# One order for three units behind each layer norm, and the last head pair scaled like the others

## The reference, cut to what matters

```python
# layer 0: gated short convolution, layer 1: forgetting attention
x = layer_norm(ALPHA * x + y)                      # y: mixer output, x @ w_out or o @ w_o
x = layer_norm(ALPHA * x + (silu(x @ w_g) * (x @ w_u)) @ w_down)
# between the layers, from the same x:
k, v = split(x @ kv_w);  logf = log_sigmoid(x @ f_w + f_b);  q = x @ w_q
# attention, per head: s = q.k/sqrt(64) + C[t] - C[s], causal; p = softmax(s); o = p @ v
```

## Time and profile before

| | us |
|---|---|
| median of 3 runs (2813.22 to 2816.91) | 2814.33 |
| profiled execution, its own time | 2815.04 |
| its span, first to last instruction | 2813.4 |
| TensorE busy in it | 2633.8 (94%) |
| VectorE, GpSimd, ScalarE busy | 1168.8, 840.6, 797.7 |
| mean granted TensorE clock | 0.968 |

### The profile page before, as it was taken

How to read it: one execution, slowest core, us unless ns; L and a number is a source line. 1 busy time by engine, 2 the same in 40 slices (tenths; PEclk the granted TensorE clock), 3 DMA queues, 4 the chain that set the end, 5 groups by cost and what they waited for, 6 DMA issues and landing times.

```text
span 2813.4 us, 44488 instructions
## 1 busy us (share of the span) xinstructions
PE 2633.8 (94%) x16651; PEld 2564.1 (91%) x16651; DVE 1168.8 (42%) x2280; ACT 797.7 (28%) x1491; POOL 840.6 (30%) x500
## 2 busy tenths in 40 slices
PE   8999979999999999878999899888899999999995
PEld 8999968999999999868999788778899999999984
DVE  2222374422222222575255677745532222222247
ACT  3111134111111111253222667632511111111114
POOL 2222244222222222243322666713522222222222
PEclk9999989999999999989999999989899999999996
DMA  3111111111111111104478877621111111111101
GB/s 115 45 45 45 45 32 38 46 46 47 51 47 46 46 46 45 32 23 143 152 263 295 254 209 207 191 72 46 31 46 46 46 46 52 46 46 46 46 31 61
DMA packets 203060, 225.92 MB, mean 80 GB/s; under 512 B 13223, under 2 KB 168871, under 8 KB 201884
## 3 DMA queue, kind: packets, MB, share of 16 engines
q1 hardware_dynamic: 194748, 190.40, 22.0%
q0 software_dynamic: 8160, 33.30, 3.7%
HBM read 182.43 MB, written 41.26 MB: 80 GB/s over the span
## 4 chain that ended last, share of the span: by engine, by line
PE 77%; DVE 10%; issue 4%; DMA 4%; ACT 2%; POOL 2%; SPq 1%; POOLq 0%; DVEq 0%; ACTq 0%
PE ps L2157 24%; PE ps L2158 24%; PE ps L2159 24%; DVE ln_d L1630 2%; DVE ln_t L1688 2%; DVE ln_t L1692 1%; PE ps L2498 1%; DMA o_t<-oe 1%; DMA ncb<-ccum 1%; DVE x L1793 1%; PE ps L2483 1%; PE ps L2480 1%; DVE ln_s L1638 1%; PE ps L2516 1%; ACT ln_y L1130 1%
## 5 line engine op out<-in xcount | busy, mean ns | idle before, releaser
L2157 PE MATMUL ps<-xh,whi 128*128 128x344 f32 x3264 | 1056.2, 324 | 50.5 <-issue 38.9
L2158 PE MATMUL ps<-xl,whi 128*128 128x344 f32 x3264 | 1049.5, 322 | 1.7 <-issue 1.7
L2159 PE MATMUL ps<-xh,wlo 128*128 128x344 f32 x3264 | 1048.7, 321 | 0.0
L765 POOL TENSOR_TENSOR wlo<-wraw,whi 128x1024 fp32r<-128x1024 f32 x196 | 468.3, 2394 | 1604.9 <-ACT whi L1049 1604.8
L2157 PEld LDWEIGHTS ps<-xh,whi 128*128 128x128 f32 x3264 | 619.0, 190 | 61.0 <-issue 44.1
L2158 PEld LDWEIGHTS ps<-xl,whi 128*128 128x128 f32 x3264 | 619.0, 190 | 2.8 <-issue 2.6
L2159 PEld LDWEIGHTS ps<-xh,wlo 128*128 128x128 f32 x3264 | 619.3, 190 | 0.0
L2157 PE MATMUL ps<-zh,whi 128*128 128x344 f32 x1440 | 474.5, 330 | 38.6 <-DVE x L1793 25.0
L1049 ACT ACTIVATE whi<-wraw 128x1024 fp32r<-128x1024 f32 x196 | 206.6, 1056 | 1061.5 <-DMA wraw<-ffn_w_gu 598.4
L2158 PE MATMUL ps<-zl,whi 128*128 128x344 f32 x1440 | 467.8, 325 | 0.0
L2159 PE MATMUL ps<-zh,wlo 128*128 128x344 f32 x1440 | 465.7, 323 | 0.0
(11 more groups left out here) (245 smaller groups left out, 2442.2 us busy)
## 6 DMA issues: line engine op xcount, KB each, us to landing
wraw<-ffn_w_gu SPq DMA_DIRECT2D x88, 512.0 KB, 3.8
wraw<-ffn_w_down SPq DMA_DIRECT2D x44, 512.0 KB, 3.6
kp<-cache_k SPq DMA_DIRECT2D x32, 512.0 KB, 5.9
vp<-cache_v SPq DMA_DIRECT2D x32, 512.0 KB, 5.3
wraw<-a_w_in SPq DMA_DIRECT2D x24, 512.0 KB, 3.7
q_t<-hl POOLq DMA_DIRECT2D x8, 1024.0 KB, 4.7
v_t<-vst POOLq DMA_DIRECT2D x8, 1024.0 KB, 7.6
vhl<-v_t SPq DMA_DIRECT2D x16, 512.0 KB, 6.4
```

The source lines that it names most:

```text
L765: pool.tensor_tensor(narrow(wlo[:, s, :], cols), narrow(wraw[:, s, :], cols), f32(narrow(whi[:, s, :], cols)), ALU.subtract).then_inc(w_lo, 1)
L2157: pe.matmul(out, w_h, m_h, start=start, stop=False)
L2158: pe.matmul(out, w_h, m_l, start=False, stop=False)
L2159: return pe.matmul(out, w_l, m_h, start=False, stop=stop)
```

## The change: what it does

1. `triple` is kept for the projections. Behind the three norms `skewed` takes its place: in each chunk the 24 blocks (k, unit) go in the order of k + LAG[unit], with LAG = (0, 2, 4): (0,0) (1,0) (2,0) (0,1) (3,0) (1,1) (4,0) (2,1) (0,2) (5,0) (3,1) (1,2) (6,0) (4,1) (2,2) (7,0) (5,1) (3,2) (6,1) (4,2) (7,1) (5,2) (6,2) (7,2). Unit 0 ends with the 16th block, unit 1 with the 21st, unit 2 with the 24th. The waits for weights and bank stand ahead of each unit's first block; `after` is run at each unit's end, with the same tables.
2. In the last pair `o_scale` is used as in all others, at its place behind the first group of the step. ScalarE copies the scaled lower half from `oe` (at the end of the step), GpSimd adds it to the upper one into `ost` (`last_sum`), with the page sums in the order 0, 1, sum 0, 2, sum 1, 3, then the other sums. `ost` moves to where the fifth buffer of `oraw` was, OS is 4. VectorE (block 5 on) and ScalarE (block 7) wait for all eight sums.

```diff
+LAG = (0, 2, 4)
...
-        ost = Area(ZL_AT + 7 * ROW).put("ost", [P, TP], F32)
+        ost = Area(XH_AT + OS * TP * 4).put("ost", [P, TP], F32)
...
-        OS = 5
+        OS = 4
... GpSimd
+            def last_sum(st):
+                e, j = st // STEPS, st % STEPS
+                cols = slice(j * 2 * P, (j + 1) * 2 * P)
+                pool.wait_ge(sm["o"], PPB * (KB - 1) + min(st + 2, PPB) + 2)
+                if st:
+                    pool.wait_ge(at["osum"], st)
+                pool.wait_ge(at["ohalf"], st + 1)
+                pool.tensor_tensor(ost[e * DH:(e + 1) * DH, cols], oe[e][0:DH, cols], otmp[:, st % 2, :], ALU.add).then_inc(at["osum"], 1)
+            sample_values(KB - 1, 0)
+            sample_values(KB - 1, 1)
+            for st in range(PAIR):
+                last_sum(st)
+                if st + 2 < PPB:
+                    pool.wait_ge(at["osum"], st + 1)
+                    sample_values(KB - 1, st + 2)
+            pool.wait_ge(at["osum"], PAIR)
... ScalarE
             def o_half(st):
-                act.wait_ge(at["ofull"], PAIR * (KB - 1) + st + 1)
-                act.activation(otmp[:, st % 2, :], ps[DH:P, 6 + st % 2, 0:2 * P], ACT.Copy).then_inc(at["ohalf"], 1)
+                e, j = st // STEPS, st % STEPS
+                if st >= 2:
+                    act.wait_ge(at["osum"], st - 1)
+                act.wait_ge(at["odone"], 2 + PAIR * (KB - 1) + st + 1)
+                act.activation(otmp[:, st % 2, :], oe[e][DH:P, j * 2 * P:(j + 1) * 2 * P], ACT.Copy).then_inc(at["ohalf"], 1)
... VectorE, step()
-                    if g == 0 and st >= 2 and not last:
+                    if g == 0 and st >= 2:
                         o_scale(b, st - 2)
-                    if g == 2 and st >= 2 and last:
-                        o_sum(st - 2)
... VectorE, behind the last pair
-            o_sum(PAIR - 1)
+            o_scale(KB - 1, PAIR - 1)
             for m in range(3, KB - 1):
                 if m == 5:
-                    dve.wait_ge(at["odone"], 2 + PAIR * KB)
+                    dve.wait_ge(at["osum"], PAIR)
... TensorE
+            def skewed(n, g, after, ready, extra=None):
+                order = sorted(((k, u) for u in range(NCH) for k in range(KB)), key=lambda ku: (ku[0] + LAG[ku[1]], ku[1]))
+                for c in range(NCH):
+                    for k, u in order:
+                        sw = (n + u) % WR
+                        wh, wl = (xhi, xlo) if u == extra else (whi[:, sw, :], wlo[:, sw, :])
+                        if k == 0:
+                            if c == 0:
+                                pe.wait_ge(w_hi, n + u + 1)
+                                pe.wait_ge(w_lo, n + u + 1)
+                            pe.wait_ge(free[u], g + c)
+                        if u == 0:
+                            ready(c, k)
+                        mm = passes(...)
+                        if k == KB - 1:
+                            mm.then_inc(full[u], 1)
+                            for what in after.get((c, u), ()):
+                                what()
...
-                triple(n0, g0, xh, xl, ln_second_part(2 * l), ready)
+                skewed(n0, g0, ln_second_part(2 * l), ready)
...
-            triple(SLOTS["f"], UNITS["f"], xh, xl,
+            skewed(SLOTS["f"], UNITS["f"],
```

More of the change, by code:

```diff
@@ L1014, in _ @@
             add_halves(KB - 2, 1)
-            for g in range(PPB):
-                sample_values(KB - 1, g)
+            def last_sum(st):
[14 more added lines that the diff above has]
+            pool.wait_ge(at["osum"], PAIR)
             proj_low("o", 2)
@@ L1459, in step @@
                         pt_high(b, st, g)
-                    if g == 0 and last and st >= 2:
-                        o_half(st - 2)
                     if g == 0 and st >= 1:
@@ L1465, in step @@
                         exps(b, st + 2, g)
+                if last and st >= 2:
+                    o_half(st - 2)
             for t in range(2):
@@ L1505, in _ @@
                 o_high(m, oraw[:, m % OS, :])
-            act.wait_ge(at["odone"], 2 + PAIR * KB)
+            act.wait_ge(at["osum"], PAIR)
             o_high(KB - 1, ost[:, :])
@@ L2049, in o_scale @@
                 e, j = st // STEPS, st % STEPS
-                spread = dve.to_reg(s + 1)
-                summed = dve.to_reg(s + 1)
-                stored_before = dve.to_reg(16 * (b + 1))
+                spread = dve.to_reg(s + 1) if not isinstance(s, int) else s + 1
+                summed = dve.to_reg(s + 1) if not isinstance(s, int) else s + 1
+                stored_before = dve.to_reg(16 * (b + 1)) if not isinstance(b, int) else 16 * (b + 1)
                 apart(dve)
@@ L2059, in o_scale @@
                                   ALU.mult).then_inc(at["odone"], 1)
[L2061 to L2072, removed]
             def step(b, st, last=False):
@@ L2108, in _ @@
                 step(KB - 1, st, True)
-            o_sum(PAIR - 2)
+            o_scale(KB - 1, PAIR - 2)
             sample_sum(KB - 1)
@@ L2159, in passes, with triple @@
                 return pe.matmul(out, w_l, m_h, start=False, stop=stop)
-            def triple(n, g, mh, ml, after, ready=None, extra=None):
+            def triple(n, g, mh, ml, after):
                 for c in range(NCH):
@@ L2165, in triple @@
                         sw = (n + u) % WR
-                        wh, wl = (xhi, xlo) if u == extra else (whi[:, sw, :], wlo[:, sw, :])
+                        wh, wl = whi[:, sw, :], wlo[:, sw, :]
                         if c == 0:
@@ L2171, in triple @@
                         for k in range(KB):
-                            if ready is not None and u == 0:
-                                ready(c, k)
                             mm = passes(ps[:, u, 0:CH], wh[:, k * P:(k + 1) * P], wl[:, k * P:(k + 1) * P],
@@ L2178, in triple @@
                             what()
+            def skewed(n, g, after, ready, extra=None):
[11 more added lines that the diff above has]
+                            ready(c, k)
+                        mm = passes(ps[:, u, 0:CH], wh[:, k * P:(k + 1) * P], wl[:, k * P:(k + 1) * P],
+                                    sl(xh[:, k, :], c), sl(xl[:, k, :], c), k == 0, k == KB - 1)
+                        if k == KB - 1:
+                            mm.then_inc(full[u], 1)
+                            for what in after.get((c, u), ()):
+                                what()
             def ln_mean(i, c):
```

## The result

The changed kernel takes 2856.57 us (median of 4 runs, 2850.53 to 2860.55) against 2813.89 (2813.22 to 2816.91) for the one before beside it: ratio 1.0143, 95% interval 1.0125 to 1.0160, slower by 1.4%. The forecast was 2846, with 2832 to 2858 as its range; the median lies 1.4 us inside its upper end, and it is also the number that rival C gave (2856), so the total alone can't tell the two apart. The profiled execution took 2858.37 us.

The account below looks back on a forecast made before the run. TensorE, busy 94% of the span, was taken as the bound. Terms of 15.3 and 15.3 (FFNs), 11.8 (f/v/q) and -10.1 (last pair) sum to 32.3 us: forecast 2846 beside the median of 2814.33, range 2832 to 2858.

Parts of the forecast that it names:

- rival C: Whole kernel: as forecast, but the last pair gains nothing since ScalarE and GpSimd wait for each other; 2856 us, chance 0.07.
- FFN, first chunk: FFN 0, chunk 0: TensorE waits 6.4 us behind the third block for unit 1's low weights; chunk 1 starts 8.3 us later.
- FFN, size: Each of FFN 0 and FFN 1: the skewed order costs 15.3 us, bounds 12 to 18.
- The chain of the norm: FFN: the norm's matmuls hang on the ends of units, unit 0 now ending after 16 blocks; `dsum` comes 8.3 us later.
- the lag: FFN, chunk 1: the fourth block waits for `free[1]` with 21 blocks remaining, not 16; 2.4 us, not paid again in chunk 2.
- half clock: FFN: TensorE at half rate costs 2.1 us before `ln_bc(1)` and 1.2 us after the wait for the fourth unit's weights.
- f/v/q: f/v/q units: late low weights of unit 2 delay unit 0's end and `first_f(0)`; 11.8 us slower, bounds 9.5 to 14.
- The last head pair: Last head pair of attention: falls to the other pair's pace with the new `o_scale`; -10.1 us, between -6 and -13.
- ScalarE's and GpSimd's loop: Last pair: GpSimd's adds gate ScalarE's `o_half` two steps later; if it waits each time, 5 of the gain are gone.
- The ring and the late half: End of attention: with OS = 4 loads wait for `o_low(0)`, and `o_half(7)` waits for `o_scale(7)`; block 6 comes 1.7 us later.
- A: Whole kernel: low weights are there when the third block ends, so TensorE's waits in the triples go; 2790 us, chance 0.06.
- B: Whole kernel: weights late but the norm's chain not, only the five-block lags and weight ring count; +4, 2818 us, chance 0.07.

Follow-up runs that it names:

- Detaching it alone: Changed kernel with the norm's matmuls placed by block counts, ScalarE's first gate and VectorE's first f moved back: 2830.18 us, ratio 1.0047 to the kernel before.
- early weights alone: Changed kernel with the late low weights made earlier on GpSimd and the high ones on ScalarE: 2840.64 us, ratio 1.0086 to the kernel before.
- the kernel nearest to it: Changed kernel with both low weights made earlier and the norm's matmuls placed by block counts: 2827.67 us, ratio 1.0028 to the kernel before.
- the last pair alone: Changed kernel with the three triples in the old block order, so only the last head pair differs from the kernel before: 2808.42 us, ratio 0.9968 to it.
- the skew alone: Kernel before with the skewed order at the three places and the old last pair: 2864.47 us, ratio 1.0177 to the kernel before.

## Why the prediction was right, and where a size was off

The cause was named as the runs show it: the lead of unit 0 meets late low weights after three blocks, and the norm's matmuls and the heads of two queues hang on unit 0's end.

- **FFN, first chunk: right.** Forecast and trace: idle behind the third block 6.4 and 6.36; `ln_bc(1)` 430.8 and 430.40; the variance matmuls behind `dsum` 437.9 and 437.66; chunk 1 at 444.7 and 444.8; the fourth block of it 450.0 and 449.74; the wait for the fourth unit's weights 3.4 and 3.56.
- **FFN, size: 15.3 forecast, 17 to 18 found** (17.9 and 17.1), inside the bounds of 12 to 18. The chain of the norm is not the part that was off: 8.3 forecast, 8.5 found at FFN 0. Two parts are: the lag was said not to be paid twice, but chunk 2 waits 1.10 us again, at every FFN that had the skew there; and 3.3 us were reckoned for half clock, where 5.1 came.
- **f/v/q: 11.8 forecast, 14.6 to 17.0 found**; this is the term that was mis-sized, beyond its bound of 14. Counted from the start of the triple, `first_f(0)` ran 1.3 us later than forecast, since the eight blocks behind the wait took 6.6 us for 5.5; chunk 1 began 1.0 us later and its fourth block 1.5. The 13 blocks from there to `ln_bc(2)` were put at 6.1 us, full clock, and took 8.6: the first of them ran at half clock until 1273.5, and TensorE had waited 3.78 and 2.42 us just before. With that VectorE's scaling of chunk 2 came late, and the wait for `first_f(1)`, which I let move with it at 10.6, moved by 15. I had allowed half clock once behind the first wait and 1.2 us for all others.
- **The last head pair: -10.1 forecast, -9.0 (-14 to -3) found** by the ratio of the kernel that has it alone. Steps 1 to 7 were to fall by 11.4 us; they fell by 13.3 in the changed kernel and 11.2 in that one. ScalarE's and GpSimd's loop didn't bind: the adds took 0.72 us, inside the bounds given. The ring and the late half cost 1.6 us in the tail (1.7 forecast), with the 2.09 us that ScalarE waits for `o_scale(7)` where said; behind that its waits for loads are 0.11 us at most in the changed kernel, so there the late half costs it and the ring next to nothing.
- **The two effects.** The chain of the norm was called the larger one. Detaching it alone gave 27 us, early weights alone 16 and both 32. The runs bear that out with a limit: some 11 us belong to both, and the early weights were early enough only at f/v/q.
- **The rivals.** A fell in the changed kernel, where its condition, the weights there at the third block, did not hold; whether the skew would pay with all of them in time no run shows, and the kernel nearest to it was 17 us above the last pair alone. B fell with the skew alone. C, with 2856, named the total best, and fell with the last pair alone: the total was met for another reason, larger costs of the skew beside a gain in the last pair.
- **Readings that were off.** Of the "five more blocks of unit 0 whose x was there" three had no low part of x yet when the wait began. Behind the variance matmuls at 429.63 not 24 blocks were ready but the eight of unit 2 of chunk 0 and at most three of chunk 1; order is kept there all the same. And 2814.33 and 32.3 make 2847, not 2846. None of this changes a term of the sum.
- **Order kept.** TensorE stood 6.36 us with blocks of unit 0 queued behind unit 1's first, two of them ready at once and all five by 419.4; the trace agrees once more with the Trainium skill, page "TensorE: Matmul & The Clock Gate", section "Part 2: What happens when you issue a matmul".

The sum, 32.3, was 8 us too small by the ratio and 10 by the medians. In the traces the two sizes at the three places make 9.6. So the mechanism was forecast and is shown; that the total stayed inside the range, by 1.4 us, is in part luck, since one term had left its bounds and the range held it only because the bounds of all terms had been added up.

## What to carry to other kernels

When an order is spread over several accumulations, the leading one ends late; look up everything that is hung on its end (matmuls of another chain, the head of each reader's queue, the slot of its weights, its bank) before counting what the spreading may win. A side chain that needs a few matmuls should be tied to when its inputs are ready, not to the end of a unit: with the skewed order that gave 27 us. With the old order it is 2 to 3 us a place in the traces, which the medians don't resolve. And price every new wait of a few microseconds with the half clock behind it, each one, not once per place.

## What the runs showed of the hardware that was not expected

- The clock can fall after the wait is over. In the changed kernel's FFN 0 the passes behind the wait of 1.89 us (0.43 us for the first) ran at full rate for 1.1 us and then, with no idle time between, at half, one each 0.29 us, until 454.3, and from there one each 0.16:

```profile
451.01 0.49 PE L2163 MATMUL ps<-xl,whi 128*128 128x344 f32 x1
451.29 0.49 PE L2164 MATMUL ps<-xh,wlo 128*128 128x344 f32 x1
...
454.69 0.32 PE L2162 MATMUL ps<-xh,whi 128*128 128x344 f32 x1
454.85 0.32 PE L2163 MATMUL ps<-xl,whi 128*128 128x344 f32 x1
```

- Other passes in the first 3.4 us of a wait of 6 had the clock at full right behind it (first pass 0.39 us for 0.62), but for 1.4 us only; in the traces 1 to 2 us were won per place, and nothing in the median.
- The same pair of heads, the sixth, took 33.4 us in one profile and 40.9 in another of nearly the same program, so one pair of profiles can't price a change of 5 us there: the 5.6 us that the pairs ahead seemed to lose are no more than such a difference.
